# Both buffers of split weights start 32 bytes behind a multiple of 64

## The reference, cut to what matters

```python
def swiglu(x, w_gate, w_up, w_down):
    return (jax.nn.silu(x @ w_gate) * (x @ w_up)) @ w_down

# first block (1 layer), then second block (2 layers), per layer:
h = h + 0.5 * g1 * swiglu(u, w_ff1_gate, w_ff1_up, w_ff1_down)    # feed-forward
h = h + g2 * token_mixing(u, w_in, ..., w_br_gla, w_br_moba, w_out)
h = h + 0.5 * g3 * swiglu(u, w_ff2_gate, w_ff2_up, w_ff2_down)    # feed-forward
```

## The kernel before, in words

| stage | lines | products | moving, upper part | moving, lower part |
|---|---|---|---|---|
| up stages of five feed-forward layers, and the projections into the mixers | L1747-1749 | 2304 | `uhi` | `ulo` |
| down stages of all six layers | L1747-1749 | 1056 | `hhi` | `hlo` |
| two branch products of the first mixer, and the outputs of mixers 1 and 2 | L1747-1749 | 192 | `mix_hi` | `mix_lo` |
| output of mixer 0 | L1747-1749 | 64 | `merged_a` | `merged_a`, `merged_b` |
| up stage of layer 1 and two chunks of mixer 0 ("shift tiles", 258 columns for the upper part) | L1785-1787 | 384 | `uhi` with a stride of 258 | `ulo` |
| tiles by token (values of the mixers), where the activation is stationary and the weights move | L1845-1847, L1834-1836 | 160 | `whi`, `wlo` | `whi` |

## Time and profile before

### The profile page before, as it was taken

The page is one execution under the profiler, slowest core; times in us unless marked ns, Lnnn a source line. Parts: engine busy times, 40 slices in busy tenths (PEclk is TensorE's granted clock), DMA queues, the critical chain, the costliest instruction groups (busy, mean ns, idle before and its releaser), DMA issues.

```text
span 1631.0 us, 33740 instructions
## 1 busy us (share of the span) xinstructions
PE 1606.9 (99%) x13569; PEld 1569.1 (96%) x13569; DVE 1150.0 (71%) x1470; ACT 801.6 (49%) x973; POOL 172.9 (11%) x193
## 2 busy tenths in 40 slices
PE   6999999999999999999999999999999999999999
PEld 4999998999999999999999999999999999999999
DVE  6877789878766657666688876656665588776653
ACT  3444445355544455444565654445444465554442
POOL 1100114600000000000053200000000035200000
PEclk9999999999999999999999999999999999999999
DMA  9998897746666477755744566568665764456653
GB/s 333 309 310 249 242 334 231 226 156 194 183 187 186 131 194 203 195 164 160 231 142 130 155 179 183 151 182 220 193 183 146 205 192 130 130 167 189 170 160 115
DMA packets 501553, 315.60 MB, mean 193 GB/s; under 512 B 14816, under 2 KB 489675, under 8 KB 501451
## 3 DMA queue, kind: packets, MB, share of 16 engines
q1 hardware_dynamic: 491824, 282.33, 60.7%
q0 software_dynamic: 8496, 29.92, 5.2%
q10 hardware_dynamic: 1130, 1.90, 0.3%
HBM read 313.04 MB, written 1.05 MB: 193 GB/s over the span
## 4 chain that ended last, share of the span: by engine, by line
PE 73%; DVE 3%; ACT 1%; issue 0%; ACTq 0%; DVEq 0%
PE accs L1747 20%; PE accs L1749 20%; PE accs L1748 19%; PE accs L1785 1%; PE wide L1785 1%; PE wide L1787 1%; PE accs L1787 1%; PE wide L1786 1%; PE accs L1786 1%; DVE wlo L1057 1%; PE wide L2018 1%; PE accs L1845 1%; PE accs L1846 1%; PE accs L1847 1%; PE bank L2089 0%
## 5 line engine op out<-in xcount | busy, mean ns | idle before, releaser
L1747 PE MATMUL accs<-uhi_room,whi 128*128 128x256 f32 x2304 | 651.8, 283 | 3.0 <-DVE ulo L1108 1.2
L1749 PE MATMUL accs<-uhi_room,wlo 128*128 128x256 f32 x2304 | 646.4, 281 | 0.0
L1748 PE MATMUL accs<-ulo,whi 128*128 128x256 f32 x2304 | 644.4, 280 | 0.0
L746 ACT CAST whi<-raw 128x2048 fp32r<-128x2048 f32 (+2 forms) x294 | 500.0, 1703 | 106.1 <-PE accs L1749 58.8
L1057 DVE TENSOR_TENSOR wlo<-raw,whi 128x2048 fp32r<-128x2048 f32 (+2 forms) x249 | 496.3, 2001 | 4.1 <-ACT gat L984 3.1
L1747 PEld LDWEIGHTS accs<-uhi_room,whi 128*128 128x128 f32 x2304 | 435.7, 189 | 11.3 <-issue 5.2
L1748 PEld LDWEIGHTS accs<-ulo,whi 128*128 128x128 f32 x2304 | 432.1, 188 | 1.2 <-issue 1.2
L1749 PEld LDWEIGHTS accs<-uhi_room,wlo 128*128 128x128 f32 x2304 | 433.2, 188 | 0.0
L1747 PE MATMUL accs<-hhi_room,whi 128*128 128x256 f32 x1056 | 295.7, 280 | 0.9 <-DVE wlo L1057 0.8
L1748 PE MATMUL accs<-hlo_room,whi 128*128 128x256 f32 x1056 | 295.5, 280 | 0.0
L1749 PE MATMUL accs<-hhi_room,wlo 128*128 128x256 f32 x1056 | 294.8, 279 | 0.0
(11 more groups left out here) (357 smaller groups left out, 2230.9 us busy)
## 6 DMA issues: line engine op xcount, KB each, us to landing
raw<-in_ffn_w_in SPq DMA_DIRECT2D x176, 512.0 KB, 5.1
in_turn<-in_w_ada POOLq DMA_DIRECT2D x56, 512.0 KB, 5.5
raw<-in_w_mix_in SPq DMA_DIRECT2D x52, 512.0 KB, 4.7
raw<-in_ffn_w_out SPq DMA_DIRECT2D x64, 384.0 KB, 3.6
raw<-in_w_ff_gate SPq DMA_DIRECT2D x44, 512.0 KB, 4.4
raw<-in_w_ff_up SPq DMA_DIRECT2D x44, 512.0 KB, 6.3
raw<-in_w_in SPq DMA_DIRECT2D x40, 512.0 KB, 4.9
raw<-in_ffn_w_out SPq DMA_DIRECT2D x64, 320.0 KB, 4.1
```

The source lines that it names most:

```text
L746: nc.scalar.copy(whi[:, n % RING, 0:cols], raw[:, n % RING, 0:cols]).then_inc(hi_ready, 1)
L1747: mm(dst, wh, xh, start=first, stop=False)
L1748: mm(dst, wh, xl, start=False, stop=False)
L1749: return mm(dst, wl, xh, start=False, stop=last)
```

## The change

Eight unused floats (32 bytes) are put ahead of `whi`, and eight behind `wlo`. Both buffers, and all tiles in them, so start 32 bytes over a multiple of 64, where they started on one. Everything from `h` on is moved up by 64 bytes, so its distance from a multiple of 64 stays. A filler of 192 bytes ahead of `lb` makes the whole displacement 256 bytes for all that is declared after it (`intra`, `toe`, `hhi`, `hlo`, `mix_hi`, `merged`, the attention's tiles). `ada_first`, which uses the place of the weight buffers in the first microseconds, moves with them. No instruction is added, removed or reordered on any engine; only addresses differ.

```diff
@@ -178,11 +178,13 @@
         raw = sb("raw", [P, RING, SLOT])
 
 
+        sb("ahead_of_weights", [P, 8])
         early = ExitStack()
         ada_first = early.enter_context(nc.sbuf_tensor("ada_first", [P, 2 * RING, SLOT], F32))
         early.close()
         whi = sb("whi", [P, RING, SLOT], F32R)
         wlo = sb("wlo", [P, RING, SLOT], F32R)
+        sb("behind_weights", [P, 8])
         h = sb("h", [P, KD, T])
@@ -232,6 +234,7 @@
         fbias = sb("fbias", [8, 2])
+        sb("filler", [P, 48])
         lb = sb("lb", [P, 8])
```

## The result

The changed kernel takes 1639.35 us in the median of six runs (1638.72 to 1641.49), the kernel before 1631.34 us in six (1629.42 to 1632.9). The ratio is 1.0043, with a 95% interval of 1.0031 to 1.0055: 8.0 us slower. The forecast was 1645.7 us. It had the direction and the larger of its two main terms, that of the down stages; the other, that of the up stages, did not come at all.

What follows compares the result with a forecast made beforehand. PE was taken to bound the kernel: number of matmuls times distance between starts. Terms 7.7 + 8.8 - 0.6 - 0.6 + 0.5 - 1.3 = +14.5 us gave 1645.7 us against the median; eight-in-ten range 1620 to 1652 us.

Steps and rivals of the forecast that it cites:

- What bounds the kernel: Whole kernel: PE sets the time, number of matmuls times distance between starts; no other engine or DMA sets the end.
- Down stages, +8.8 us: 1056 products go from no equal start of load and stream to three, 351.7 to 360.0 ns: +8.8 us.
- Up stages, +7.7 us: Up stages and projections, 2304 products: steps with equal starts over 64 go from one to two, +3.3 ns each: +7.7 us.
- a rule over 64: All stages: 350 ns a product, plus 3.3 ns per step where load and stream start at the same place over 64.
- only the down stages fall: Rival: down stages take the slow pace, up stages keep 353.4 ns: +6.8 us, 1638 us; chance 0.13.
- Branch products and mixer outputs, -0.6: Branch products and outputs of mixers 1 and 2, 192 products: three equal starts to none, 353.4 to 350.0 ns, -0.6 us.
- Output of mixer 0, -0.6: Output of mixer 0, 64 products: three equal starts of load and stream to none, -10.0 ns each, -0.6 us.
- Shift tiles, -1.3: Shift tiles, 384 products: the equal start under `ulo` goes, -3.3 ns each, -1.3 us.
- Tiles by token, +0.5: Tiles by token, 160 products: steps with equal starts go from one to two, +0.5 us.
- The place doesn't matter: Rival: the two paces are the array's own; up stages stay, down stages -1.8 to +1.9 us, 1629 to 1633 us; chance 0.22.
- Two tiles both on a multiple of 64: Rival: only both tiles on such a start cost, so every slow step goes: -10.8 us, 1620 us; faster overall 0.25.
- Every stage slow: Rival: every stage falls into the slow pace, +23.3 us, 1654.5 us; chance 0.07.

Runs made afterwards that it cites:

- Run 1: Changed kernel with `hhi` and `hlo` moved another 32 bytes, so weights and hidden tiles are 32 bytes apart again: 1629.04 us, ratio 0.9982.
- run 15: The kernel before, unchanged, profiled once more: 1633.1 us.
- Run 6: Changed kernel with the whole 256-byte displacement put directly behind the weights, so `uhi` is at 160 and `ulo` at 128 over 256: 1646.84 us, ratio 1.0087.
- Run 7: Changed kernel (weights at 160 over 256) with the hidden tiles of the six down stages at six pairs of places over 256: 1635.57 us.
- run 2: The kernel before with `ulo` moved from 0 to 32 over a multiple of 64: 1626.78 us, ratio 0.9961.
- run 9: Changed kernel (weights at 160 over 256) with `uhi`, `ulo`, `hhi`, `hlo` all at 192, 32 bytes behind the weights: 1626.29 us, ratio 0.9961.
- run 3: The kernel before with `hhi` and `hlo` alike at 0, 8, 16, 24, 40, 48 over 64 in the six down stages: 1639.72 us.
- run 5: The kernel before (weights at 128 over 256) with the hidden tiles of the six down stages at six pairs of places over 256: 1634.79 us.
- run 10: The kernel before with `whi` alone moved to 160 over 256, `wlo` left at 128: 1631.76 us.
- run 11: The kernel before with `wlo` alone moved to 160 over 256, `whi` left at 128: 1640.75 us, ratio 1.0044.
- run 16: The changed kernel, unchanged, profiled once more: 1639.53 us.
- run 4: The kernel before with `hhi` and `hlo` at unlike places over 64, a different pair in each of the six down stages: 1632.81 us.
- run 17: The kernel before with upper parts of weights and activations at 128 over 256 and lower parts at 160: 1630.93 us, ratio 0.9996.
- Run 12: Run 2's kernel with mixers' and merged tiles at 160, and two idle 512-column matmuls ahead of each of two waits: 1629.43 us, ratio 0.9976 against before.

## Why the prediction was right or wrong

- **What bounds the kernel: right.** PE's starts decide, and they moved with the places of loads and streams. The other engines' times and the waits stayed, as costed; nothing in the transfers answers for the difference.
- **Down stages, +8.8 us: right,** measured +8.6. The pace of mixer 0's output carried over to other tiles that share a place over 256. Run 1 undoes it with 32 bytes. The value of before, 351.7, was a mean over two paces that a stage may take differently in another execution (run 15), so part of the agreement to 0.2 us is luck.
- **Up stages, +7.7 us: wrong, measured 0,** and this is the step that failed. The prediction said: "Load and stream now meet in two steps (weights 32, `uhi` 32)". They are equal over 64 only; over 256 they are 160 and 224. The table ahead of the prediction has both figures, and the down stages were judged by the second one ("all four tiles stand at 160") while the up stages were judged by the first. Run 6 makes the places what the sentence assumed, and there the up stages cost 355.9 ns and the kernel 1646.84 us. Run 7 has the real pair and the assumed pair side by side in one execution, 353.4 and 356.0. So for the places that were assumed the term had the right sign and was somewhat too large (356.0 ns a product for 357); the change didn't give these places.
- **The warning was there.** The output of mixer 1 had spoken against a rule over 64: equal over 64, unlike over 256, 353.4 ns. The prediction noted it, and used it for the rival "only the down stages fall", at 1638 us and a chance of 0.13. That rival was the case (1639.35 us). Weighing it above the forecast needed no new row, only the same measure for both terms.
- **Branch products and mixer outputs, -0.6: wrong in sign,** +0.6 us (356.6 for 353.5). The same fault again: the change also moved `mix_lo` from 0 to 64 over 256. Run 6, with `mix_lo` at 0, has 351.1 to 351.4 ns, near the 350 of the forecast. Why the 64 bytes cost 5 ns a product stays open.
- **Output of mixer 0, -0.6: right in sign,** -0.3 us; its loads fell from 192 to 189 ns but the product kept 354.9.
- **Shift tiles, -1.3: right in sign,** -0.7 us. **Tiles by token, +0.5:** the pace went the way that was said in mixer 0 (353.6 to 356.4) and hardly in the others (354.1 to 354.5); +0.2 us or so.
- **The rivals.** "The place doesn't matter" is refuted: runs 1, 2, 6 and 9 move the median from 1626.3 to 1646.8 us with addresses alone. The Trainium skill, page "SBUF — State Buffer", section "Who interferes with whom", gives TensorE's moving operand and its weight loads read ports of their own, independent of one another; here the loads take 188 or 192 ns and a product 350 or 360 by where the two start, so the runs don't bear out that the two have no effect on one another. What they share no run shows. "Two tiles both on a multiple of 64" is refuted by the down stages of after, with no tile on one. "Every stage slow" didn't come.

What remains open: why a given set of places has its pace. The rule of meetings over 64 fails in runs 3 and 5, over 256 it fails in runs 3 (360 and 363 with nothing equal), 7 (360 with only `hhi` equal), 10 and 11. So equal places over 256 were enough for the slow pace wherever they were tried, and they are not the only way to it.

Some sets kept their pace in every profile that had them: all tiles at one place over 256, 359.5 to 360.0 ns; the pair of after's up stages, 353.3 to 353.4 in the stages of the layers (after, runs 1, 7 and 16); that of before's up stages with both weight buffers at 128, 353.3 to 353.4 (before, runs 3, 4, 5 and 15); that of run 6, 355.9 to 356.0 (and in run 7). Moving tiles 32 behind the weights ran at 350.0 mostly and at up to 353.3 in some stages.

## What to carry to other kernels

Where a kernel is bound by PE's starts, with a weight load beside every short stream as here, the start addresses of stationary and moving tiles within 256 bytes are a parameter worth some tenths of a per cent, and 1.3% between the extremes of this case (1626.3 and 1646.8 us): measure it by starts in the timeline, stage by stage, and compare all tiles over the same modulus. Keep loaded and moving tiles off the same place over 256, but don't take any other distance for safe: with `hhi` 24 and 40 bytes behind the weights and `hlo` 64 further, run 3 had 360 and 363 ns. All moving tiles 32 bytes behind the weights was the best that held here (0.9961 [0.9945, 0.9976] in runs 2 and 9). A "harmless" padding ahead of one buffer moves every tile declared behind it, so its cost or gain can lie in a stage that the change doesn't speak of.

## What the runs showed of the hardware that was not expected

**Paces come in steps, mostly.** Most undisturbed stretches lie at 346.7, 350.0, 353.3, 356.7, 360.0 or 363 ns a product, 3.3 ns apart, which at 2.4 GHz is 8 cycles. Not all do: run 6's up stages hold 356.0, and other sets have means between the steps. The same instructions and addresses can hold two of them (before: 350.0 and 353.3; run 17: 346.7 and 353.3), and a stage may change from one to the other and stay: before's first down stage runs its first chunks at 350 and its last six at 353.4, in both profiles.

**Short stretches at half clock, in some executions.** The granted clock was 0.5 for 3.4 or 6.8 us at a time; before's first profile has none in its body, its second (run 15) has two; 13 of the 19 profiles of this case have one or two. In run 2 (us, PE busy and matmuls, granted clock, DMA share, GB/s; below it the timeline):

```profile
200.00:207.00 7.00, 6.10 (x53) 1.00 1.02 317
207.00:214.00 7.00, 7.00 (x35) 0.51 1.05 331
214.00:221.00 7.00, 7.00 (x62) 1.00 0.24 71
```
```profile
204.68 0.28 PE L1750 MATMUL accs<-hhi_room,wlo 128*128 128x256 f32 x1
205.86 2.55 PE L1854 MATMUL bank<-ones,intra 128*128 128x1 f32 x16 [0.90 <-DVE intra L1234]
208.27 0.56 PE L1748 MATMUL accs<-hhi_room,whi 128*128 128x256 f32 x1
208.63 0.41 PE L1749 MATMUL accs<-hlo_room,whi 128*128 128x256 f32 x1
208.84 0.41 PE L1750 MATMUL accs<-hhi_room,wlo 128*128 128x256 f32 x1
209.06 0.41 PE L1748 MATMUL accs<-hhi_room,whi 128*128 128x256 f32 x1
```

The engine had waited 0.90 us and done sixteen matmuls of one column; the clock fell to half during these, at 207.0 us, and the steps after it are 0.21 us instead of 0.117, at 1.2 GHz, and 35 matmuls fit where 62 do at 2.4 GHz. In the profile of after there were two such stretches, one from 210.0 us and one from 250.9 us; the first:

```profile
210.40:213.80 3.40, 3.40 (x19) 0.56 1.09 334
213.80:220.80 7.00, 7.00 (x61) 1.00 0.46 147
```

By the halved pace (0.21 us a step for 0.117) a stretch of 3.4 us full of matmuls costs some 1.5 us, an estimate; the two of after cost some 2.2 together, since fewer matmuls fell into the second. They bear on how executions of one kernel differ: of the seventeen of before that stand beside run 1, the seven with a mean granted clock of 1.0 took 1629.79 to 1631.26 us and the six with 0.996 to 0.998 took 1633.89 to 1637.93. Run 9 holds its 1622.5 us of span with two of them. That a wait brings them on is a reading of where most of them lie, and is not shown: before's first profile has the same waits and none. Run 12, which filled waits at 208 and 244 us, had none at the first place, where other profiles have one, and still had one from 249.5 us; one profile can't tell whether the fill did it.
